# Token groups of 2, 3 and 3 tiles, one expert pipeline beside all later stages, and tensor-engine sums in the last stretch only

## The chip, the core and the metric

The kernel runs on one core of a Trainium2 chip. The metric is the device time of one execution, in microseconds (us), from the first to the last instruction of the program with what lies around it; lower is better. The core has a tensor engine (PE, with its weight loads shown as PEld), a vector engine (DVE), a scalar engine (ACT), GpSimd (POOL) and SyncE (SP). In this kernel SP issues the plain transfers and POOL the indirect ones (gathers); 16 DMA engines carry both.

## What is computed

One step of a one-layer decoder for 1024 prompt tokens and 8 sampled tokens, all in 32-bit floats, model width 1024:

```
n  = RMSNorm(x)
qa,ka,va, qb,fb,ib,gb, ga,gbr = split(n @ w_in)
oa = post(softmax(q0 k0) - lam * softmax(q1 k1)) @ va      # causal, 4 heads, two maps each
ob = HGRN2 scan over chunks of tokens, 4 heads, with its own norm and gate
h  = x + (sigmoid(ga) * (oa @ w_a) + sigmoid(gbr) * (ob @ w_b)) @ w_out
x2 = RMSNorm(h)
q  = x2 @ w_query                                          # 8 heads, two halves of 64
s1,i1 = top16(q[...,0] . keys0); s2,i2 = top16(q[...,1] . keys1)
cs,ci = top16(all sums s1 + s2); idx = 128 * i1 + i2; w = softmax(cs)
h  = h + sum over 8*16 slots of  w * gelu(x2 . expert_u[idx]) * expert_v[idx]
y  = RMSNorm(h)
```

The last part, here called the experts, needs 128 rows of `expert_u` and `expert_v` for each token. With 128 tokens to a tile, one *slot* is one such row for every token of a tile: a gather of 128 rows of 2048 numbers (8 KB, u and v side by side), a dot product with x2, a gelu, and a weighted sum into h.

## The kernel before

The 1032 tokens are nine tiles: eight of 128 prompt tokens and one of the eight sampled tokens. `GROUPS` (L47) makes two groups of them, tiles 0 to 3 (a) and 4 to 8 (b). `program` (L2267) runs a list of stages for each group, one after the other, with a barrier of all engines between stages (`Stage.end`, L161):

- `normalise` (L170), once for all tokens.
- `project` (L342): 16 column chunks of w_in with the tokens as the moving operand (L476), each chunk loaded into one of two buffers, then row blocks v, i, g with the weights as the moving operand (L488). Group b's 520 tokens go in two slices of 260.
- `attend_prompt` (L499), for b `attend_sample` (L705), `hgrn` (L898), `hgrn_out` (L1145), `merge` (L1303).
- For group a, `fronts` (L1878): for each of its four tiles h, x2, the queries and the ranking. The ranking runs on the vector engine: five passes of MAX8, FIND_INDEX8 and MATCH_REPLACE8 over 16 score lists, the same over eight lists of sums, then one-hot products that turn positions into row numbers (L1792 to L1865). Tiles 0 to 2 stay in SBUF, tile 3 is written out ("handed").

Slots are worked in two places. `Side` (L1429) works the 384 slots of tiles 0 to 2 beside all stages of group b. `SHARES` (L2339) says what percentage of them each stage takes: 18 project, 31 attend_prompt, 15 attend_sample, 20 hgrn, 3 hgrn_out, 13 merge. In each stage the engines call `side.dve(done, total)` and its like after each step of their own, and so many slots are issued there as are due. One slot is a gather on POOL (L1485), a dot product (L1556) on the vector engine, a gelu and a scaling on the scalar engine (L1498, L1500), and a sum on the vector engine two slots later (L1522). Eight ring buffers hold gathered rows; POOL waits before each gather until the sum of eight slots earlier is done.

`experts` (L1940) then works the 640 slots of tiles 3 to 7 in a loop over tiles, and eight slots for the sampled tokens behind it. Here the vector engine makes a diagonal matrix of each slot's coefficients (L2176) and the tensor engine sums, two products of 128x512 for each slot (L2073). All steps of the following tile's front (from `Front`, L1580) are placed between the slots by a list of slot numbers (`slots_with_front`), so ranking, w_out and w_query lie beside the gathers:

```
AT_H, AT_ADD, AT_ROOT, AT_N2, AT_N2T, AT_Q, AT_QN, AT_QT, AT_S = (1, 3), 5, 7, 9, 11, (13, 15), 16, 18, 20
AT_KEYS, AT_COMB, AT_BEST, AT_EXP, AT_ROWS, AT_IDX, AT_W = 23, 34, 36, 47, 49, 59, 60
```

Of the kernel before, what the change touches and what calls it, by code (L numbers as in the profile page):

```python
# [13 lines left out]
P = 128  # L20
# [30 lines left out]
GROUPS = ((0, 4), (4, NT))  # L51


N_BESIDE = 3

ARENA = 50400
# [70 lines left out]
class Group:  # L127


    def __init__(self, name, lo, hi):  # L130
        self.name, self.lo, self.hi = name, lo, hi
        self.tiles = range(lo, hi)
        self.prompt = range(lo, min(hi, NP))
        self.t0 = lo * P
        self.n = min(hi * P, T) - self.t0
        self.np = len(self.prompt) * P
        width = -(-self.n // -(-self.n // 512))
        self.slices = [(a, min(width, self.n - a)) for a in range(0, self.n, width)]
        self.sampled = hi == NT

HANDED = 2 * D + 2 * SLOTS


def parts_of(handed):
    return {"h": handed[:, 0:D], "n2": handed[:, D:2 * D], "idx": handed[:, 2 * D:2 * D + SLOTS].bitcast(U32),
            "w": handed[:, 2 * D + SLOTS:HANDED]}

# [192 lines left out]
def project(nc, top, io, c, g, side):  # L342
# [3 lines left out]
    qk, v_all, ident = c["qk"], c["v"], c["ident"]  # L346
    with ExitStack() as st:
# [4 lines left out]
        wn = [m.sb(f"wn{u}", [P, KD, 512]) for u in range(1 if g.lo else 2)]  # L352
        row_st = [m.sb(f"row_st{u}", [P, 512]) for u in range(2)]
        col_st = m.sb("col_st", [P, g.n])
        pt = [[banks.ps(f"pt{g.name}{u}_{s}", [P, 512]) for s in range(len(g.slices))] for u in range(2)]
# [21 lines left out]
        NSL = len(g.slices)  # L377
# [13 lines left out]
        def _(sp):  # L391
# [5 lines left out]
            for k in range(2, N_COLS):  # L397
                load_w(sp, k)
                if k > n_direct + 1:
                    sp.wait_ge(cols_stored, NSL * (k - 1))  # L400
                    sp.dma_start(io["hqf"][k - 2 - n_direct][:, g.t0:g.t0 + g.n], col_st).then_inc(cols_saved, 16)
            for k in range(N_COLS - 2, N_COLS):
                sp.wait_ge(cols_stored, NSL * (k + 1))
# [27 lines left out]
        def _(act):  # L431
            for k in range(N_COLS):
# [3 lines left out]
                for s, (a, n) in enumerate(g.slices):  # L436
                    dst = qk[:, k, g.t0 + a:g.t0 + a + n] if k < n_direct else col_st[:, a:a + n]
                    last = nc.scalar.copy(dst, pt[k % 2][s][:, 0:n])
                    last.then_inc(cols_stored, 1)
# [18 lines left out]
        @block.vector  # L458
        def _(dve):
            side.dve(1, 1)  # L460
# [6 lines left out]
        def _(pe):  # L467
            pe.wait_ge(xnt_landed, 16)
            for k in range(N_COLS):
                u = k % 2  # L470
                if k >= 2:
                    pe.wait_ge(cols_stored, NSL * (k - 1))
                pe.wait_ge(wt_landed[u], 16 * (k // 2 + 1))
                for d in range(KD):
                    for s, (a, n) in enumerate(g.slices):
                        last = nc.tensor.matmul(pt[u][s][:, 0:n], wt[u][:, d, :], xnt[:, d, a:a + n],  # L476
                                                start=(d == 0), stop=(d == KD - 1))
                last.then_inc(cols_done, 1)
            for n, (b, t) in enumerate(items):
# [10 lines left out]
                else:  # L490
                    pe.wait_ge(cols_stored, NSL * N_COLS)
                    c0 = CK if b == "k" else CQ
                    for h in range(H):
                        last = nc.tensor.transpose(out[0:rows(t), h * P:(h + 1) * P],
                                                   qk[:, c0 + h, t * P:t * P + rows(t)], ident[:])
                last.then_inc(rows_done, 1)


def attend_prompt(nc, top, io, c, g, side):  # L499

    qk, v_all, ident = c["qk"], c["v"], c["ident"]
    units = [(i, h) for i in g.prompt for h in range(H)]
    NG = len(g.prompt)
    with ExitStack() as st:
# [9 lines left out]
        NSC = 2 if len(g.prompt) + g.lo <= NP // 2 else 1  # L514
        sc = [[banks.ps(g.name + f"sc{b}{k}", [P, SEQ // NSC]) for k in range(2)] for b in range(NSC)]
        pt = banks.ps(g.name + "at_pt", [P, SEQ])
        o_ps = banks.ps(g.name + "o_ps", [P, H, DV])
        ot_ps = banks.ps(g.name + "ot_ps", [P, H, P])
# [19 lines left out]
        def _(pe):  # L538
            def scores(u):
                i, h = units[u]  # L540
                w = (i + 1) * P
                for k in range(2):
# [3 lines left out]
                    for k0 in range(0, w, 512):  # L546
                        n = min(512, w - k0)
                        last = nc.tensor.matmul(sc[u % NSC][k][:, k0:k0 + n],  # L548
                                                qk[k * DH:(k + 1) * DH, CQ + h, i * P:(i + 1) * P],
                                                qk[k * DH:(k + 1) * DH, CK + h, k0:k0 + n],  # L550
# [3 lines left out]
            def turn(u):  # L554
                i, h = units[u]
                pe.wait_ge(diff_ready, u + 1)
                if u >= 1:
                    pe.wait_ge(probt_ready, u)
                for b in range(i + 1):
                    last = nc.tensor.transpose(pt[:, b * P:(b + 1) * P], prob[u % 2][0][:, b * P:(b + 1) * P],  # L560
                                               ident[:])
                last.then_inc(turned, 1)

            def pv(u):
                i, h = units[u]
                pe.wait_ge(probt_ready, u + 1)
# [7 lines left out]
            def turn_out(i):  # L574
                pe.wait_ge(on_ready, i + 1)
                if i >= 1:
                    pe.wait_ge(oat_stored, i)
# [6 lines left out]
            for u in range(len(units)):  # L584
# [3 lines left out]
                pv(u)  # L588
                if u % H == 0 and u:
# [4 lines left out]
        def _(act):  # L594
            def exps(u):
                w = (units[u][0] + 1) * P
                for k in range(2):
                    q = 2 * u + k
                    act.wait_ge(neg_ready, u + 1)
                    if u >= 2:  # L600

                        act.wait_ge(turned, u - 1)
# [4 lines left out]
            def store(u):  # L607
                w = (units[u][0] + 1) * P
                act.wait_ge(turned, u + 1)
                if u >= 1:  # L610
                    act.wait_ge(pv_done, u)
                nc.scalar.copy(probt[:, 0:w], pt[:, 0:w]).then_inc(probt_ready, 1)
# [92 lines left out]
def attend_sample(nc, top, io, c, g, side):  # L705
# [5 lines left out]
    with ExitStack() as st:  # L711
# [20 lines left out]
        w_ps = banks.ps("w_ps", [P, PAGES, NS * H])  # L732
        ow_ps = banks.ps("ow_ps", [NS, NS * H])
        o_ps = banks.ps("as_o_ps", [NS * H, H, DV])
        f_ps = banks.ps("as_f_ps", [P, 512])
# [33 lines left out]
        def _(pool):  # L769
            for n in range(2 * NS):  # L770
# [14 lines left out]
                side.pool(n, 2 * NS)  # L785
            side.pool(1, 1)

        @block.tensor
        def _(pe):
            for b in range(NS):  # L790
                if b >= 1:
# [4 lines left out]
                                 ).then_inc(q_spread, 1)  # L796
            pe.wait_ge(s_ready, 1)
# [9 lines left out]
            nc.tensor.matmul(ow_ps[:], pown[:], c["sum_maps"][:], start=True, stop=True).then_inc(w_done, 1)  # L807
# [37 lines left out]
        def _(dve):  # L845
# [34 lines left out]
            link(v.tensor_copy(own_w[:], ow_ps[:]))  # L880
# [17 lines left out]
def hgrn(nc, top, io, c, g, side):  # L898
# [8 lines left out]
    with ExitStack() as st:  # L907
# [12 lines left out]
        tp = [banks.ps(g.name + f"hg_tp{b}", [P, 4, P]) for b in range(2)]  # L920
# [1487 lines left out]
```

## Time and profile before

| | us |
|---|---|
| three runs | 4554.89, 4537.21, 4544.08; median 4544.08 |
| the profiled execution, span | 4543.0 |
| vector engine busy in it | 2761.8 (61%) |
| tensor engine busy in it | 2851.9 (63%) |
| queue of the gathers, share of 16 DMA engines | 62.7% |

The span of the profiled execution is the time from its first to its last instruction; nothing else of that execution is shown, and it lies 1.1 us under the median of the three runs. A busy time is the union of an engine's instructions. The profile's slices and windows show that no engine is busy all the time: each stage has its own limit, so the rows below are cut by stage.

### The profile page before, as it was taken

What the parts mean: (1) busy time and instruction counts of PE and PEld (TensorE: products, weight loads), DVE (VectorE), ACT (ScalarE), POOL (GpSimd) and SP (SyncE); (2) the same over time, 40 slices, a digit from 0 to 9 for tenths busy, and PEclk for the clock granted to TensorE, in tenths of its full rate; (3) what the DMA queues carried; (4) which work ended last, traced back from release to release, by engine and by line L of the source; (5) the groups of instructions that cost most, each with busy time, mean ns of one, the idle gap of its engine ahead of it and who ended that gap; (6) DMA issues with size and microseconds to landing.
All of it is one profiled execution on the core that took longest, in us unless ns stands there. A gap on an engine that the chain in (4) does not pass through costs nothing. (4 is left out here: it accounts for less than half of the span.)

```text
span 4543.0 us, 27167 instructions
## 1 busy us (share of the span) xinstructions
PE 2851.9 (63%) x7469; PEld 1351.7 (30%) x7469; DVE 2761.8 (61%) x5875; ACT 770.2 (17%) x1942; POOL 1419.0 (31%) x1130
## 2 busy tenths in 40 slices
PE   6964696529722322322286676787777777778777
PEld 3432233217211110011175232332233233222222
DVE  1044114966479989799656457557646755755673
ACT  1035101101134421244233000000010000001000
POOL 0000000014345557544223234333333333342441
PEclk9976798759866655655588898988899889888987
DMA  5201422049779888988687988889989988987995
GB/s 178 84 26 32 153 75 73 10 161 349 260 305 357 343 306 324 364 314 324 223 315 314 376 344 342 339 339 353 351 320 352 367 331 341 354 343 312 348 350 216
DMA packets 228998, 1245.86 MB, mean 274 GB/s; under 512 B 26040, under 2 KB 56376, under 8 KB 95104
## 3 DMA queue, kind: packets, MB, share of 16 engines
q0 software_dynamic: 153728, 1098.98, 62.7%
q1 hardware_dynamic: 75136, 145.37, 8.9%
q8 instruction: 50, 0.82, 0.1%
q14 instruction: 84, 0.69, 0.0%
HBM read 1210.87 MB, written 33.39 MB: 274 GB/s over the span
## 5 line engine op out<-in xcount | busy, mean ns | idle before, releaser
L2073 PE MATMUL x_acc<-arena 128*128 128x512 f32 x2560 | 1334.6, 676 | 531.7 <-DVE arena L2176 531.4
L2184 DVE CUSTOM_DVE_ANT_0 arena<-arena 128x1024 f32<-128x1024 f32 x640 | 777.2, 1222 | 736.6 <-DMA arena<-in_experts,arena 727.1
L2025 POOL DMA_INDIRECT arena<-in_experts,arena x648 | 751.7, 1160 | 1250.5 <-PE x_acc L2073 1087.5
L1485 POOL DMA_INDIRECT arena<-in_experts,arena x384 | 594.5, 1548 | 1752.3 <-POOLq L163 969.0
L2073 PEld LDWEIGHTS x_acc<-arena 128*128 128x128 f32 x2560 | 531.9, 216 | 1321.2 <-DVE arena L2176 709.3
L1522 DVE SCALAR_TENSOR_TENSOR arena<-arena 128x1024 f32<-128x1024 f32 x384 | 491.3, 1280 | 127.6 <-ACT arena L1500 127.4
L1556 DVE CUSTOM_DVE_ANT_0 arena<-arena 128x1024 f32<-128x1024 f32 x384 | 467.6, 1218 | 36.4 <-DMA arena<-in_experts,arena 34.7
L2138 ACT ACTIVATE arena<-arena 128x2 f32<-128x2 f32 x320 | 65.1, 203 | 1765.0 <-DVE arena L2184 1764.9
L2176 DVE TENSOR_SCALAR arena<-ident,arena 128x128 f32<-128x128 f32 x640 | 191.2, 341 | 0.0
L476 PE MATMUL ptb<-arena 128*128 128x260 f32 x512 | 116.4, 387 | 97.2 <-DMA arena<-in_w_t 97.1
L1498 ACT ACTIVATE arena<-arena 128x1 f32<-128x1 f32 x384 | 77.3, 201 | 547.8 <-DVE arena L1556 526.4
L644 DVE TENSOR_TENSOR a_sc<-a_sc,cmask 128x128 f32<-128x128 f32 x32 | 7.9, 293 | 241.9 <-PE a_sc L548 241.9
L560 PE MATMUL b_at_pt<-ident,arena 128*128 128x128 f32 x104 | 26.4, 429 | 197.0 <-DVE arena L662 197.0
L1664 PE MATMUL x_a_ps<-arena 128*128 128x512 f32 (+1 forms) x320 | 140.6, 592 | 0.0
L1374 PE MATMUL b_mg_ps<-arena 128*128 128x260 f32 x512 | 119.4, 387 | 25.9 <-DMA arena<-in_wb 25.9
L1664 PE MATMUL a_f_a_ps<-arena 128*128 128x512 f32 x256 | 122.6, 639 | 18.2 <-DMA arena<-in_norm 13.4
L476 PEld LDWEIGHTS ptb<-arena 128*128 128x128 f32 x512 | 97.2, 191 | 116.1 <-issue 98.6
L1374 PE MATMUL a_mg_ps<-arena 128*128 128x512 f32 x256 | 115.3, 603 | 24.1 <-DMA arena<-in_wb 24.1
L488 PE MATMUL pnb<-arena 128*128 128x512 f32 (+1 forms) x240 | 109.8, 618 | 25.9 <-DMA arena<-in_w_n 25.9
L476 PE MATMUL pta<-arena 128*128 128x512 f32 x256 | 112.1, 599 | 16.7 <-DMA arena<-in_w_t 16.7
L1404 DVE TENSOR_TENSOR arena<-arena,a_mb_ps 128x512 f32<-128x512 f32 x8 | 5.5, 687 | 183.1 <-ACT arena L1389 183.1
L1500 ACT ACTIVATE arena<-arena 128x1 f32<-128x1 f32 x384 | 113.1, 295 | 12.8
(365 smaller groups left out, 3102.3 us busy)
## 6 DMA issues: line engine op xcount, KB each, us to landing
arena<-in_w_t SPq DMA_DIRECT2D x64, 512.0 KB
arena<-in_experts,arena POOLq DMA_INDIRECT x1032
arena<-in_w_n SPq DMA_DIRECT2D x6, 2048.0 KB, 12.1
arena<-in_w_out SPq DMA_DIRECT2D x2, 4096.0 KB, 12.9
arena<-in_w_query SPq DMA_DIRECT2D x2, 4096.0 KB
arena<-xnt_scratch SPq DMA_DIRECT2D x2, 2080.0 KB
arena<-in_x SPq DMA_DIRECT2D x4, 1024.0 KB
xnt_scratch<-arena SPq DMA_DIRECT2D x8, 512.0 KB, 4.2
```

The costliest lines, as they stand in the source:

```text
L476: last = nc.tensor.matmul(pt[u][s][:, 0:n], wt[u][:, d, :], xnt[:, d, a:a + n], start=(d == 0), stop=(d == KD - 1))
L488: last = nc.tensor.matmul(out[0:rows(t), :], xnt[:, d, a:a + rows(t)], wn[u][:, d, :], start=(d == 0), stop=(d == KD - 1))
L1374: nc.tensor.matmul(g_ps[q % 2][x][:, 0:n], wg[u][x][:, d, :], xnt[:, d, t0:t0 + n], start=(d == 0), stop=(d == KD - 1))
L1485: pool.indirect_dma_start(out=c["ring"][:, s0 % RING, :], out_offset=None, in_=self.io["experts"], in_offset=bass.IndirectOffsetOnAxis(ap= ...
L1500: act.activation(c["coef"][:, r], c["dots"][:, r], ACT.Copy, scale=c["first_w"][:, i, s0:s0 + 1]).then_inc(self.coef_ready, 1)
L1522: dve.scalar_tensor_tensor(out=h, in0=c["ring"][:, r, D:2 * D], scalar=c["coef"][:, r:r + 1], in1=h, op0=ALU.mult, op1=ALU.add).then_inc(s ...
L1556: dve.tensor_tensor_reduce(out=u, in0=u, in1=c["first_n2"][:, i, :], scale=1.0, scalar=0.0, op0=ALU.mult, op1=ALU.add, accum_out=c["dots"] ...
L1664: last = self.nc.tensor.matmul(self.a_ps[0:R, n * 512:(n + 1) * 512], lhs[:, k, 0:R], rhs[:, k, n * 512:(n + 1) * 512], start=(k == 0), st ...
L2025: nc.gpsimd.indirect_dma_start(out=ring[:, r, :], out_offset=None, in_=io["experts"], in_offset=bass.IndirectOffsetOnAxis(ap=rows_at, axis ...
L2073: last = nc.tensor.matmul(acc[:, n * 512:(n + 1) * 512], diag[:, s % RING, :], ring[:, s % RING, D + n * 512:D + (n + 1) * 512], start=(s ...
L2176: v.tensor_scalar(diag[:, s % RING, :], ident[:], gel[:, s % RING:s % RING + 1], w_cur[:, s:s + 1], ALU.mult, ALU.mult).then_inc(diag_read ...
L2184: ins = v.tensor_tensor_reduce(out=ring[:, r, 0:D], in0=ring[:, r, 0:D], in1=n2_cur[:], scale=1.0, scalar=0.0, op0=ALU.mult, op1=ALU.add, ...
```

## The change

Groups become tiles 0 and 1 (a, 256 tokens), 2 to 4 (b, 384) and 5 to 8 (c, 392), each in one slice. w_in, w_a, w_b, w_out and w_query are therefore read once for each of three groups. `fronts` and `experts` are gone. Each group gets two more stages: `hidden` (h and x2 for all its tiles, w_out in 16 chunks of 256 KB) and `rank` (w_query in eight chunks, then the same ranking passes, 20 steps to a tile, in the same order). h, x2, row numbers and weights of every tile are written out to `handed`. The sampled tokens' eight slots get a stage of their own, `experts_sample`.

A single pipeline, `Experts`, works all 1024 prompt slots in order of tiles; two SBUF buffers hold a tile's h, x2, numbers and weights, loaded by POOL in front of the tile's first gather. `PLAN` gives the number of slots beside each stage: 20 in a's `rank`, once tile 0 is ranked; 282 in group b; 389 in group c; the other 333 in a stage `rest` at the end, where nothing else runs. The second number is the share of slots that the tensor engine sums: 0 beside all stages (the vector engine sums them, as `Side` did), 0.7 in `rest`. For those the scalar engine now makes the diagonal matrix. Attention's transposes use one PSUM bank instead of two, four blocks at a time, and `project` has two buffers for row-block weights in every group.

```diff
-GROUPS = ((0, 4), (4, NT))
+GROUPS = ((0, 2), (2, 5), (5, NT))
...
-SHARES = {False: {project: 32, attend_prompt: 26, hgrn: 18, hgrn_out: 2, merge: 22},
-          True: {project: 18, attend_prompt: 31, attend_sample: 15, hgrn: 20, hgrn_out: 3, merge: 13}}
+PLAN = (
+    {rank: (20, 0.0)},
+    {project: (50, 0.0), attend_prompt: (34, 0.0), hgrn: (46, 0.0), hgrn_out: (6, 0.0), merge: (36, 0.0),
+     hidden: (20, 0.0), rank: (90, 0.0)},
+    {project: (62, 0.0), attend_prompt: (60, 0.0), attend_sample: (30, 0.0), hgrn: (46, 0.0), hgrn_out: (8, 0.0),
+     merge: (46, 0.0), hidden: (25, 0.0), rank: (100, 0.0), experts_sample: (12, 0.0), rest: (NP * SLOTS, 0.7)},
+)
...
+    def pool(self, done, total):
+        pool, c = self.nc.gpsimd, self.c
+        to = self.due(done, total)
+        if to:
+            to = min(self.N, to + RING - self.PE_LAG)
+        for b in range(self.at["pool"], to):
...
+            if s == 0:
+                pool.wait_ge(self.tile_landed[i % 2], 16 * (i // 2 + 1))
+            if b >= RING:
+                if self.by_pe[b - RING]:
+                    pool.wait_ge(self.pe_used, self.pe_to[b - RING + 1])
+                else:
+                    pool.wait_ge(self.dve_used, self.dve_to[b - RING + 1])
+            pool.indirect_dma_start(
...
+            if s == self.AT_LOAD and i + 1 < NP:
+                self.load(i + 1)
...
+    def act(self, done, total):
...
+            act.wait_ge(self.dots_ready, b + 1)
+            act.activation(c["dots"][:, r], c["dots"][:, r], ACT.Gelu).then_inc(self.gel_ready, 1)
+            act.wait_ge(self.gel_ready, b + 1)
+            act.activation(c["coef"][:, r], c["dots"][:, r], ACT.Copy, scale=w).then_inc(self.coef_ready, 1)
+            if self.by_pe[b]:
+                act.wait_ge(self.coef_ready, b + 1)
+                act.activation(c["diag"][:, b % RING, :], c["ident"][:], ACT.Copy, scale=c["coef"][:, r]
+                               ).then_inc(self.diag_ready, 1)
...
+            for r in range(NR):
+                R = rows(g.lo + r)
+                for n in range(STEPS):
+                    if n < 5:
+                        keys_top(n, r, R)
+                    elif n == 5:
+                        combine(r, R)
+                    elif n < 11:
+                        best_top(n - 6, r, R)
...
+                    side.dve(*point(HP + STEPS * r + n + 1))
```

How the vector engine's order changes in the ranking: L1792, L1794 and L1796 are its MAX, MAX_INDEX and MATCH_REPLACE passes (L1643, L1645, L1647 in the changed kernel). An ISA row is a slot's dot product (its second row reads the accumulator out). Before, in the expert loop, tile 4's ranking stood like this:

```order
L1792 MAX arena<-x_s_ps 128x8 x16
L2184 ISA arena<-arena 128x1024
L2184 ISA arena 128x1
L2184 ISA arena<-arena 128x1024
L2184 ISA arena 128x1
L2176 TENSOR_SCALAR arena<-ident,arena 128x128 x2
L2184 ISA arena<-arena 128x1024
L2184 ISA arena 128x1
L2184 ISA arena<-arena 128x1024
L2184 ISA arena 128x1
L2176 TENSOR_SCALAR arena<-ident,arena 128x128 x2
L1794 MAX_INDEX arena<-arena,x_s_ps 128x8 x16
```

In the changed kernel, in the `rank` stage of group b:

```order
L1643 MAX arena<-b_rk_s 128x8 x16
L2125 ISA arena<-arena 128x1024
L2125 ISA arena 128x1
L2078 SCALAR_TENSOR_TENSOR arena<-arena 128x1024
L1645 MAX_INDEX arena<-arena,b_rk_s 128x8 x16
L2125 ISA arena<-arena 128x1024
L2125 ISA arena 128x1
L2078 SCALAR_TENSOR_TENSOR arena<-arena 128x1024
```

Four slots stood between two passes, each with a dot product and a short diagonal (two to a batch); now one slot or two, each with a dot product and a full-width sum (L2078).

The second place is POOL's queue in `rest`, with the gathers (L2003), a tile's load (L1978) and the store of a finished tile (L1983):

```order
L1875 UNCONDITIONAL_BRANCH
L2003 DMA arena<-in_experts,arena 128x2048 x71
L1978 DMA arena<-handed_scratch 128x2304
L2003 DMA arena<-in_experts,arena 128x2048 x41
L1983 DMA y<-arena 128x1024
L2003 DMA arena<-in_experts,arena 128x2048 x87
L1978 DMA arena<-handed_scratch 128x2304
```

Loads and stores of tiles, which SP issued before, now stand between the gathers, and the first gather of a tile waits for its load.

## Rows read from the trace of the kernel before

**Rows 1.** The page's part 1 (busy time of each engine) and two lines of part 2.

```profile
PE 2851.9 (63%) x7469; PEld 1351.7 (30%) x7469; DVE 2761.8 (61%) x5875; ACT 770.2 (17%) x1942; POOL 1419.0 (31%) x1130
...
DMA  5201422049779888988687988889989988987995
GB/s 178 84 26 32 153 75 73 10 161 349 260 305 357 343 306 324 364 314 324 223 315 314 376 344 342 339 339 353 351 320 352 367 331 341 354 343 312 348 350 216
```

**Rows 2.** Windows, one per stage: from:to us, length, engines' busy us (x), PEclk, DMA share, GB/s.

```profile
0.00:41.30 41.30, 11.52 (x72) 9.99 (x72) 19.35 (x38) 14.15 (x24) 5.77 (x24) 0.96 0.66 209
41.30:255.00 213.70, 197.23 (x464) 87.20 (x464) 0.00 (x0) 18.66 (x32) 0.00 (x0) 0.96 0.32 108
255.00:342.60 87.60, 51.51 (x200) 30.17 (x200) 50.16 (x152) 37.19 (x95) 0.00 (x0) 0.64 0.04 13
342.60:485.50 142.90, 60.35 (x256) 32.71 (x256) 63.38 (x136) 69.80 (x136) 0.00 (x0) 0.67 0.13 39
485.50:678.00 192.50, 167.92 (x384) 73.35 (x384) 15.82 (x24) 9.97 (x17) 0.00 (x0) 0.93 0.33 120
678.00:975.80 297.80, 142.86 (x448) 68.91 (x448) 222.94 (x856) 26.49 (x34) 0.00 (x0) 0.73 0.11 38
975.80:1297.50 321.70, 231.08 (x776) 142.23 (x776) 164.41 (x208) 52.20 (x194) 120.70 (x76) 0.86 0.85 320
1297.50:1675.00 377.50, 114.41 (x456) 76.51 (x456) 358.43 (x517) 153.24 (x365) 189.73 (x120) 0.59 0.86 336
1675.00:1909.30 234.30, 79.78 (x119) 21.34 (x119) 193.99 (x238) 39.13 (x132) 155.12 (x122) 0.59 0.87 332
1909.30:2272.40 363.10, 96.83 (x340) 46.56 (x340) 293.99 (x453) 136.40 (x340) 133.26 (x89) 0.54 0.78 285
2272.40:2477.50 205.10, 170.78 (x768) 146.89 (x768) 134.47 (x196) 76.59 (x160) 59.11 (x41) 0.92 0.81 310
2477.50:4480.00 2002.50, 1484.58 (x3116) 602.79 (x3117) 1228.07 (x3021) 128.21 (x396) 747.84 (x650) 0.89 0.89 344
4480.00:4543.00 63.00, 43.09 (x71) 13.01 (x69) 16.76 (x36) 8.17 (x17) 7.49 (x8) 0.65 0.35 142
```

**Rows 3.** Timeline, vector engine, beside the attention: start us, us, instruction.

```profile
1310.10 1.22 DVE L1556 CUSTOM_DVE_ANT_0 arena<-arena 128x1024 f32<-128x1024 f32 x1
...
1311.24 1.28 DVE L1522 SCALAR_TENSOR_TENSOR arena<-arena 128x1024 f32<-128x1024 f32 x1
1312.44 1.22 DVE L1556 CUSTOM_DVE_ANT_0 arena<-arena 128x1024 f32<-128x1024 f32 x1
```

**Rows 4.** Costliest groups of the page: busy us, mean ns | idle before, releaser.

```profile
L2184 DVE CUSTOM_DVE_ANT_0 arena<-arena 128x1024 f32<-128x1024 f32 x640 | 777.2, 1222 | 736.6 <-DMA arena<-in_experts,arena 727.1
L2025 POOL DMA_INDIRECT arena<-in_experts,arena x648 | 751.7, 1160 | 1250.5 <-PE x_acc L2073 1087.5
L1485 POOL DMA_INDIRECT arena<-in_experts,arena x384 | 594.5, 1548 | 1752.3 <-POOLq L163 969.0
```

**Rows 5.** Groups by line and form, tensor engine: the projections' two passes.

```profile
L476 PE MATMUL ptb<-arena 128*128 128x260 f32 x512 | 116.4, 387 | 97.2 <-DMA arena<-in_w_t 97.1
...
L476 PE MATMUL pta<-arena 128*128 128x512 f32 x256 | 112.1, 599 | 16.7 <-DMA arena<-in_w_t 16.7
...
L488 PE MATMUL pnb<-arena 128*128 128x512 f32 x192 | 88.9, 625 | 25.9 <-DMA arena<-in_w_n 25.9
```

**Rows 6.** DMA: the gathers' queue (packets, MB, share), and two issues (KB, us to landing).

```profile
q0 software_dynamic: 153728, 1098.98, 62.7%
...
xnt_scratch<-arena SPq DMA_DIRECT2D x8, 512.0 KB, 4.2
...
arena<-handed_scratch SPq DMA_DIRECT2D x1, 1152.0 KB, 5.1
```

**Rows 7.** Timeline, vector engine, `fronts`: first and last instruction of four tiles' ranking.

```profile
731.76 0.89 DVE L1792 MAX8 arena<-a_f_s_ps 128x8 f32<-128x128 f32 x4 [24.61 <-PE a_f_s_ps L1711]
...
970.66 0.29 DVE L1865 TENSOR_TENSOR arena<-arena 128x128 f32<-128x128 f32 x1
```

More of the change, by code:

```diff
@@ new lines, in pe, with pe_end, pe_slots @@
+    def pe(self, done, total):
+        self.pe_slots(self.due(done, total) - self.PE_LAG)
+    def pe_end(self):
+        self.pe_slots(self.N)
+    def pe_slots(self, to):
+        pe, c = self.nc.tensor, self.c
+        for b in range(self.at["pe"], to):
+            if not self.by_pe[b]:
+                continue
+            i = b // SLOTS
+            first = self.pe_to[b] == self.pe_to[i * SLOTS]
+            last = self.pe_to[b + 1] == self.pe_to[(i + 1) * SLOTS]
+            if first and i:
+                pe.wait_ge(self.acc_taken, i)
+            pe.wait_ge(self.diag_ready, self.pe_to[b + 1])
+            for n in range(2):
+                ins = pe.matmul(self.acc[:, n * 512:(n + 1) * 512], c["diag"][:, b % RING, :],
+                                c["ring"][:, b % RING, D + n * 512:D + (n + 1) * 512], start=first, stop=last)
+            ins.then_inc(self.pe_used, 1)
+        self.at["pe"] = max(self.at["pe"], to)
@@ L2319, in program @@
+        c["free"] = kept.at
+        groups = [Group("abc"[n] + "_", lo, hi) for n, (lo, hi) in enumerate(GROUPS)]
+        experts = Experts(nc, c, io, acc, [PLAN[n][build] for n, g in enumerate(groups) for build in BUILDS
+                                           if build in PLAN[n]])
+        for n, g in enumerate(groups):
             for build in BUILDS:
-                if build is attend_sample and not g.sampled:
+                if build in (attend_sample, experts_sample, rest) and not g.sampled:
@@ L2321, in program @@
                     continue
-                beside.stage(build)
-                stage(nc, build, io, c, g, beside)
-            if n:
-                beside.sems.end()
-            if not g.sampled:
-                c["free"] = kept.at
-                handed = g.hi - 1 if GROUPS[n + 1][1] == NT else None
-                stage(nc, fronts, io, c, g, handed)
-                tiles = range(g.lo, g.hi if handed is None else handed)
-                beside = Side(nc, c, io, tiles, GROUPS[n + 1][1] == NT)
@@ new lines, in program @@
+        experts.sems.end()
+BUILDS = (project, attend_prompt, attend_sample, hgrn, hgrn_out, merge, hidden, rank, experts_sample, rest)
+PLAN = (
[5 more added lines that the diff above has]
+)
```

1494 lines of the change are left out of this document (706 added, 788 removed).

## Prediction

> **What bounds the kernel now.** I read the page's shares first [rows 1]: no engine is over 63% busy in 4543.0 us, so there is no single bound and the span has to be cut. The lines of slices show why: up to slice 8 the DMA engines are mostly idle, from slice 9 on their digit is 8 or 9. The windows by stage [rows 2] give three stretches. Until 975.8 us no expert row is gathered. From there to 2477.5 (1501.7 us) group b's stages run with 384 slots beside them, 3.91 us a slot. From there on the loop works 640 slots in 2002.5 us, 3.13 each, and 63.0 us end it. Adding the windows' vector-engine times in the middle stretch gives 1145 us, 76% of it: the attention is bound by that engine (358.43 of 377.5), hgrn partly (293.99 of 363.1), `project` and `merge` by the tensor engine and by transfers (DMA share 0.85 and 0.81). In the loop the DMA share is 0.89 and the vector engine is busy for 61% only: it waits 727.1 us for gathered rows [rows 4]. The ranking of tiles 4 to 7 and the sampled tokens lies in those waits and costs little.
>
> **Prices.** A slot beside a stage costs the vector engine 2.34 us, the pitch from one dot product to the next with a sum between (1310.10 to 1312.44, [rows 3]). A slot's gather moves 128 rows of 8 KB, 1.05 MB; the gathers' queue used 62.7% of the span [rows 6], 2848 us, so at most 2.76 us of all 16 engines for each of 1032 gathers. At the loop's 344 GB/s it takes 3.05 us [rows 2]. Ranking four tiles took 731.76 to 970.95 us [rows 7], 59.8 a tile. That holds early steps of later tiles and waits; `fronts` had the vector engine busy for 222.94 us [rows 2], 56 a tile, some 3 of them early steps. I take 55 for the ranking alone, bounds 53 and 60.
>
> **Group a (256 tokens).** `normalise` stays at 41.3 [rows 2]. `project`: 213.7 with 197.23 busy; half the columns and rows, 99, plus the same 16 of start and end, plus 20, since a column chunk would take 3.5 us (half of 112.1/16, [rows 5]) and its 512 KB transfer about 4.2 [rows 6]: 135. Attention 40 (half of 87.6 is 44, the narrower half less). hgrn with its output 96, between half of 142.9 and all of it, because chains and table loads for each head don't shrink. `merge` 168/2+25 = 109. `hidden` 50: w_out's products for two tiles at 15 us, a start and a tail of 10 each. `rank`: w_query's product 35, two tiles 110, 20 slots at 2.34 (47), and 15 until the first tile's load (5.1, [rows 6]) and first gather have landed: 207. Group a: **678**, where 975.8 stood, 20 slots done.
>
> **Group b (384 tokens, 282 slots).** `project`: tensor engine 116.4·384/520 = 86 for columns plus 67 for nine row items (88.9/12 each, [rows 5]), 153, with start and a tail of slots 189; by bytes 73 MB at this stage's 320 GB/s 229; I take 205. Attention: 34 slots 80, own work 46, at the 95% of before 133, fill and drain 15: 148. Its transposes in parts of four add a handover to each unit of tiles 4 to 7, at most 1 us each, behind vector work: 0, bound 16. hgrn and output: 363.1 less 37 slots (87), one tile (20) and the sampled tokens (35, bounds 0 and 60): 221. `merge`: 170.78·384/520 = 126 plus the 34 of before is 160, by bytes 54 MB at 310 GB/s 173: 165. `hidden`: 20 slots and weights are 30 MB, 88 at about 340 GB/s; tensor engine and tail 65. `rank`: eight product steps 51, in which only 11 slots are due; then one in-order queue on the vector engine holds three tiles at 55 (165) and 79 slots (185): 401, here 398 as ranking waits are partly filled. Sum **1225**.
>
> **Group c (392 tokens, 389 slots)** by the same steps: `project` 243 (223 and 270), attention 218 (377.5/16 = 23.6 a unit, less 2.4 slots), sampled attention 185 (234.3 less 28 slots is 169; POOL now issues the last 15 expert gathers ahead of the six last cache loads, so I add 16), hgrn and output 261, `merge` 190 (163 and 207), `hidden` 105 (75 and 108), `rank` 53 + 4·55 + 91·2.34 = 486, taken as 480, `experts_sample` 80 (63.0 before, 12 slots more, its final norm beside). Sum **1762**. In b and c together 671 slots take 1570 us of the vector engine and own work some 714 (105 attention, 58 sampled, 114 hgrn, 28 merge, 392 ranking and norms, 17 sampled experts), 76% of 2987, as in the middle stretch before.
>
> **Last stretch, 333 slots.** The vector engine needs 1.2 + 0.3·1.2 = 1.5 us a slot, so transfers set the pace: bounds 2.76 (busy share) and 3.13 (whole loop); 2.9 taken, near the loop without its ranking. 966, last norm and store 10. POOL's queue now holds each tile's load, and the tile's first gather waits behind it for the landing (5.1, [rows 6]); beside stages eight gathered slots at some 4 us cover that, in the last stretch two loads cost some 6 each, 12. A finished tile's store stands 40 slots into the next tile, 20 behind its norm, and holds nothing up. Together **988**. The removed diagonals and products were off the path, as was 1334.6 us of tensor engine: nothing is credited for them. The 128x128 diagonal on the scalar engine is not in this trace; a 128x512 pass there takes 0.6 us (its copies in `project`, 18.66 us for 32), so 0.2 to 0.6, beside a 2.9 us pace: 0.
>
> Sum: 678 + 1225 + 1762 + 988 = 4653 us of a span of 4543.0; the median of the runs is 1 us above it. **Forecast 4654 us, 2.4% slower.** The gain is 298 us ahead of the gathers; the loss is that ranking seven tiles, free beside the loop's gathers, now takes 881 us for 190 slots, 4.6 each, while the stretch that is left with DMA-bound slots has an idle vector engine.
>
> [...]
>
> **Rivals.** *A, faster: slots fill the stages' waits.* If the vector engine were busy 86% of b and c instead of 76%, they would take 2284/0.86 = 2656 and the kernel 4322. It decides from 80%, where the time reaches 4521. For it: the attention reached 95%, and 881 us of ranking is one dense queue. Against it: `project` had 51%, `merge` 66%, and those are bound elsewhere. Chance 0.12. *B, no change: weights and gathers don't collide.* `project`, `merge` and `hidden` at their tensor-engine times are 189+223+160+163+60+75 = 870 instead of 996, 4527. For it: in b's columns the weights mostly kept up. Against: 310 to 320 GB/s there, near the loop's 344. Chance 0.12, half of it, with the rows' own error, beyond 0.5%. *C, slower: the ring paces the last stretch.* Each of 227 slots on the tensor engine now goes dot, gelu, scaling, diagonal, two products, POOL, with eight buffers; at 3.3 us a slot it adds 133, 4787; it decides where the chain behind a landing exceeds some 8 us, eight paces of 2.9 less 15 in flight. For it: POOL waited 1087.5 us for the tensor engine before [rows 4]. Against: it did so at a DMA share of 0.89. Chance 0.18. *D, gathers alone run faster.* With no weights beside them at the best slice's 376 GB/s [rows 1], 2.79 us a slot, 4616. Chance 0.05. [...]
>
> **How the numbers follow.** The forecast has 0.53, own range 4560 to 4770 (ranking 53 to 60, last stretch 2.76 to 3.0, `project` and `merge` between their bounds). Faster by over 0.5%, about what a measurement of this kernel can tell from no change: A, half of B, a low end of the forecast's errors, 0.20. Within 0.5%: half of B and some of the forecast, 0.10. Slower: 0.70. The range 4480 to 4830 takes in B, D and most of C and leaves out A.
>
> **What would show it.** The first gather's dot product near 575 us instead of 986; group a's end near 680, b's near 1905, c's near 3665; `rank` of b and c about 400 and 480 us with the vector engine over 90% busy and a DMA share of about 0.6; the last stretch at 2.9 us a slot, DMA share 0.9, vector engine near 55%. The forecast is wrong if b and c end before 3500 us, if ranking with slots costs less than the sum of both, or if a slot of the last stretch takes over 3.2 us.
>
> PREDICTION {"us": 4654, "low": 4480, "high": 4830, "faster": 0.20, "same": 0.10, "slower": 0.70}

## The result and the profile after

The changed kernel takes 4476.21 us (median of 4 runs, 4472.53 to 4479.68); the kernel before, timed beside it, 4549.49 (4 runs, 4537.21 to 4556.57). The ratio is 0.984, 95% interval 0.982 to 0.986: 1.6% faster, where 2.4% slower was forecast. The profiled execution has a span of 4470.8 us.

The page of the changed kernel, parts 1 to 3 in extracts, answers to [rows 1, 6]:

```profile
PE 2072.8 (46%) x5841; PEld 1043.3 (23%) x5841; DVE 3080.8 (69%) x5708; ACT 1195.0 (27%) x3247; POOL 1533.9 (34%) x1137
...
DMA  5124278778798676797878685988666699999998
GB/s 201 57 80 141 100 262 346 302 284 299 273 354 353 237 259 241 291 365 295 324 281 290 222 304 214 362 349 304 226 229 226 234 378 427 410 427 407 426 427 341
...
q0 software_dynamic: 156176, 1113.13, 64.4%
```

The end is new: between the slices of 378 and 341 GB/s six stand at 407 to 427, where no slice of before passed 376. Stage by stage, the windows of the changed kernel answer to [rows 2]. They are `project` of b, `rank` of b, `rank` of c, the last stretch whole, and its inside (from:to us, length, busy us of PE, PEld, DVE, ACT and POOL, granted clock, DMA share, GB/s):

```profile
653.10:862.30 209.20, 157.23 (x412) 80.31 (x412) 119.16 (x150) 34.76 (x128) 83.14 (x50) 0.88 0.90 351
1459.70:1866.50 406.80, 52.70 (x224) 33.75 (x224) 368.66 (x908) 58.96 (x200) 127.04 (x92) 0.56 0.71 249
3066.70:3555.40 488.70, 57.52 (x256) 35.98 (x256) 443.41 (x1149) 66.98 (x223) 156.03 (x102) 0.55 0.65 229
3619.30:4470.00 850.70, 513.18 (x908) 185.78 (x908) 550.72 (x792) 265.01 (x902) 401.53 (x332) 0.86 0.97 408
3640.00:4440.00 800.00, 497.18 (x878) 180.11 (x879) 517.91 (x748) 251.98 (x862) 386.86 (x322) 0.87 1.00 422
```

Beside the ranking the vector engine is the full one (368.66 of 406.80, 443.41 of 488.70) and the DMA share is 0.71 and 0.65; in the last stretch it is the other way round, 0.97 to 1.00 at 408 to 422 GB/s with the vector engine at 65%.

Here is the whole forecast beside the measurement. Ends are those of the last instruction of a group's stages.

| | forecast, us | measured, us |
|---|---|---|
| group a, to the end of `rank` | 678 | 652.6 |
| group b, 282 slots | 1225 | 1213 (653.1 to 1866.5) |
| group c with `experts_sample`, 389 slots | 1762 | 1752 (1867 to 3618.8) |
| last stretch, 333 slots | 988 | 851 (3619.3 to 4470) |

The three groups together missed by 46 us of 3665. Three quarters of the error, 137 us, lie in the last stretch: a slot there takes 851/333 = 2.55 us, ends included, and not 2.9. The loop of before took 3.13 for the same gather. Had its slots kept that pace, the last stretch would be 333 x (3.13 - 2.55) = 193 us longer and the change slower by about 120 us.

The rows on the gathers of the changed kernel, from 3640 to 4440 us, say what their queue waited for and how long a gather takes from its issue to its landing:

```profile
L2003 POOL DMA_INDIRECT arena<-in_experts,arena x318: 932/939/1983, 3639.5 to 4435.7; - x159
its engine sat idle before it (us, times) until:
  DVE arena L2078: 294.2, 91
...
  DMA arena<-handed_scratch: 29.3, 2
...
DMA to landing us min/median/max: 5.4/12.4/15.8
```

318 gathers in 800 us are one in 2.52 us, and a landing takes 12.4, so 12.4/2.52 = 4.9 gathers are under way on average.

### The profile page after: what moved, and what is told of

The parts are those of the page before. It is cut to its first block and busy times, and to the rows that moved or that the text cites. A ratio compares the mean times of both kernels' runs of the same rounds, so it can differ in the third digit from the quotient of the medians.

```text
span 4470.8 us, 24525 instructions
## 1 busy us (share of the span) xinstructions
PE 2072.8 (46%) x5841; PEld 1043.3 (23%) x5841; DVE 3080.8 (69%) x5708; ACT 1195.0 (27%) x3247; POOL 1533.9 (34%) x1137
## 5 line engine op out<-in xcount | busy, mean ns | idle before, releaser
L2003 POOL DMA_INDIRECT arena<-in_experts,arena x1024 | 1445.9, 1412 | 2305.4 <-DVE arena L2078 2132.7
L2078 DVE SCALAR_TENSOR_TENSOR arena<-arena 128x1024 f32<-128x1024 f32 x797 | 1019.5, 1279 | 205.6 <-ACT arena L2029 205.4
L2027 ACT ACTIVATE arena<-arena 128x1 f32<-128x1 f32 x1024 | 206.6, 202 | 1886.6 <-DVE arena L2125 1885.4
L2064 PE MATMUL e_acc<-arena 128*128 128x512 f32 x908 | 513.2, 708 | 324.7 <-ACT arena L2032 274.9
L2064 PEld LDWEIGHTS e_acc<-arena 128*128 128x128 f32 x908 | 185.8, 221 | 652.2 <-ACT arena L2032 425.7
L2029 ACT ACTIVATE arena<-arena 128x1 f32<-128x1 f32 x1024 | 301.5, 294 | 33.2
L458 PE MATMUL ptc<-arena 128*128 128x392 f32 x256 | 94.5, 528 | 243.0 <-DMA arena<-in_w_t 242.8
L458 PE MATMUL ptb<-arena 128*128 128x384 f32 x256 | 93.6, 526 | 181.7 <-DMA arena<-in_w_t 181.7
L1599 PE MATMUL c_rk_s<-arena 64*128 64x128 f32 (+1 forms) x128 | 13.2, 387 | 220.8 <-DVE zero L1657 220.2
L1346 PE MATMUL c_mg_ps<-arena 128*128 128x392 f32 x256 | 89.3, 502 | 37.2 <-DMA arena<-in_wa 37.2
L1346 PE MATMUL b_mg_ps<-arena 128*128 128x384 f32 x256 | 87.7, 495 | 28.1 <-DMA arena<-in_wa 28.1
L2032 ACT ACTIVATE arena<-ident,arena 128x128 f32<-128x128 f32 x227 | 91.1, 401 | 7.4
```

What stands on the lines that cost most here:

```text
L458: last = nc.tensor.matmul(pt[u][:, 0:g.n], wt[u][:, d, :], xnt[:, d, :], start=(d == 0), stop=(d == KD - 1))
L1346: nc.tensor.matmul(g_ps[z][:, 0:g.n], wg[u][:, d, :], xnt[:, d, :], start=(d == 0), stop=(d == KD - 1))
L1599: last = nc.tensor.matmul(s_ps[0:R, x, k, :], qt[s, k, r * P:r * P + R], keys[s, k, :], start=True, stop=True)
L2003: pool.indirect_dma_start(out=c["ring"][:, r, :], out_offset=None, in_=self.io["experts"], in_offset=bass.IndirectOffsetOnAxis(ap=self.til ...
L2027: act.activation(c["dots"][:, r], c["dots"][:, r], ACT.Gelu).then_inc(self.gel_ready, 1)
L2029: act.activation(c["coef"][:, r], c["dots"][:, r], ACT.Copy, scale=w).then_inc(self.coef_ready, 1)
```

## Experiments

Two theories of the 2.55 us. **Places:** the loop of before wasn't paced by transfers at all. Its gathers waited for free buffers of the ring of eight, which dot product, gelu, diagonal and product, in batches of two, held so long that the DMA engines ran short; the new pipeline frees a buffer sooner. **Sums:** what counts is which engine sums, the vector engine having been relieved, or loaded, by the split of 0.7. The count that ties the first theory together: if all places are always taken, places x pace = landing + holding, where holding is the time from a row's landing to its buffer's release.

### Who sums in the last stretch

```diff
-     merge: (46, 0.0), hidden: (25, 0.0), rank: (100, 0.0), experts_sample: (12, 0.0), rest: (NP * SLOTS, 0.7)},
+     merge: (46, 0.0), hidden: (25, 0.0), rank: (100, 0.0), experts_sample: (12, 0.0), rest: (NP * SLOTS, 0.0)},
```

> From the changed kernel; no slot of the last stretch is summed by the tensor engine (share 0.0 for 0.7). The vector engine then needs 2.34 us a slot, still under the 2.47 us that 128 packets of 8 KB at 309 ns take on 16 engines. Theory P: the vector engine and the transfers are both nearly full, 2.5 to 2.7 us a slot, the stretch 840 to 900. Theory S: without tensor products it gets faster or stays, 820 to 851.

The second run has 1.0 in the same place.

> From the changed kernel; the tensor engine sums nearly all slots of the last stretch (share 1.0 for 0.7). Theory P: the same number of places, so 2.5 to 2.65 us a slot, the stretch within 30 us of 851. Theory S: with the sums on the tensor engine, as in the loop before, the pace goes back towards the loop's 2.95 to 3.1 us, the stretch to 970 to 1030.

Measured, in one run each: 4479.0 us with the vector engine alone, 4466.89 with the tensor engine for all slots that may go there; before, on that chip, 4555.08. Windows inside the last stretch, of the first run and then of the second:

```profile
3640.00:4440.00 800.00, 0.00 (x0) 0.00 (x0) 771.21 (x965) 163.67 (x642) 539.65 (x323) 0.50 1.00 421
```

```profile
3640.00:4430.00 790.00, 607.46 (x1225) 211.91 (x1224) 404.06 (x648) 284.29 (x940) 311.79 (x318) 0.97 1.00 422
```

The vector engine is busy for 96% in one and 51% in the other, the DMA share is 1.00 in both, and the rate stays at 421 and 422 GB/s. The last stretch is paced by transfers, as forecast; the tensor engine's part in it is worth nothing that can be measured. By the count, a place was held for 8 x 2.52 - 15.1 = 5.0 us after the landing with the tensor engine alone (its landing stands in the last section), where the changed kernel, with its share of 0.7, has 8 x 2.52 - 12.4 = 7.8: buffers came back sooner, more gathers were under way, and the pace stayed.

### Fewer places in the last stretch

```diff
+            held = 6
+            if b >= self.N - 325:
+                if self.by_pe[b - held]:
+                    pool.wait_ge(self.pe_used, self.pe_to[b - held + 1])
+                else:
+                    pool.wait_ge(self.dve_used, self.dve_to[b - held + 1])
```

> From the changed kernel; in the last stretch alone POOL also waits until the slot six places back (not only eight) has been summed, so two ring buffers stay empty. Theory P (places in flight): the last stretch ran at 2.55 us a slot because 5.05 gathers were in flight on the mean; the loop of the kernel before had 2.9 of them and 3.13 us. Two places less leave about 3 in flight, and the stretch goes from 851 us to 980 to 1060 (2.95 to 3.2 us a slot), DMA share 0.8 to 0.9; the kernel about 4600 to 4680. Theory S (who sums): the pace came from fewer products on the tensor engine, the diagonals off the vector engine and no ranking; buffers don't matter, the stretch stays within 20 us of 851.

The second run has 5 for 6.

> As the run with six places, but five: theory P expects some 2 gathers in flight, 3.6 to 4.4 us a slot, a last stretch of 1180 to 1450 us and a DMA share of 0.55 to 0.7. Theory S expects no change from 851 us.

Measured, in one run each: 4568.57 us with six places and 4683.77 with five, 96 and 211 us of span over the changed kernel. Windows inside the last stretch with six places, and then its gathers with their landing:

```profile
3650.00:4530.00 880.00, 534.26 (x872) 191.71 (x870) 513.55 (x741) 249.30 (x853) 360.95 (x320) 0.82 0.97 380
```

```profile
L2009 POOL DMA_INDIRECT arena<-in_experts,arena x316: 932/938/1953, 3653.0 to 4529.2; - x158
...
DMA to landing us min/median/max: 5.3/9.0/12.5
```

The same two views with five:

```profile
3650.00:4630.00 980.00, 557.62 (x847) 191.62 (x848) 500.74 (x724) 243.70 (x834) 335.97 (x310) 0.79 0.88 333
```

```profile
L2009 POOL DMA_INDIRECT arena<-in_experts,arena x306: 934/941/1987, 3655.9 to 4624.5; - x153
...
DMA to landing us min/median/max: 5.4/8.0/11.2
```

The direction is that of places, the size smaller than expected. The count holds: holding is 8 x 2.52 - 12.4 = 7.8 us with eight places, 6 x 2.78 - 9.0 = 7.7 with six (316 gathers in 880 us) and 5 x 3.20 - 8.0 = 8.0 with five (306 in 980). It is the same chain each time, and what places are left after it feed the DMA engines. With five, 8.0/3.20 = 2.5 gathers are under way, and the row reads as the loop of before did: a DMA share of 0.88 and 333 GB/s, for 0.89 and 344 in [rows 2].

### The kernel before with a quicker release

```diff
-    BATCH = 2
+    BATCH = 1
...
-            return [(12 + at * 52 // NB, step) for at, step in front]
+            return [(12 + at * 52 // 64, step) for at, step in front]
...
-                    if at == b:
+                    if 2 * at + 1 == b:
```

The last two lines keep the ranking steps of the next tile at the slots where they stood.

> From the kernel before; slots of its loop go one by one instead of in pairs (batch of 1 for 2), the steps of the ranking keep their places between the slots. Theory P: a buffer comes free up to one slot earlier on each link of the chain dot, gelu, diagonal, product, so 3.4 to 4.5 gathers are in flight instead of 2.9 and the loop's 640 slots take 1650 to 1850 us instead of 2002; the kernel 4200 to 4400. Theory S: the same engines do the same work, the loop stays within 40 us of 2002.

Measured: 4258.59 us (2 runs), 0.936 of before, interval 0.933 to 0.939. The DMA view of 2600 to 4100 us, before:

```profile
GB/s 356 327 353 322 343 370 334 349 310 354 313 347 358 342 354 362 355 342 354 268 360 314 365 371 340 372 369 360 367 269 355 310 354 333 376 349 354 329 353 352
...
q0 software_dynamic: 70182, 511.00, 87.7%
q1 hardware_dynamic: 5047, 4.81, 1.0%
...
arena<-in_experts,arena POOLq DMA_INDIRECT x486
```

With batches of one:

```profile
GB/s 395 382 423 421 422 396 423 366 422 386 421 421 421 420 422 350 352 421 382 421 422 421 416 421 353 345 420 383 422 421 422 417 417 400 310 412 380 419 419 421
...
q0 software_dynamic: 82129, 598.10, 97.1%
q1 hardware_dynamic: 5184, 5.31, 1.1%
...
arena<-in_experts,arena POOLq DMA_INDIRECT x572, 11.8
```

The same loop, gathers and ranking between the slots: 572 gathers for 486, at up to 423 GB/s. The same dot products, diagonals and sums are done; each slot goes through the chain by itself and gives its buffer back by itself. That the buffers are what counts in this, and not a finer order of the work, is for the next run to show. The loop, up to where the last tile's sum is taken into h, went from 2004.5 us (2477.5 to 4482.0) to 1716.8 (2478.7 to 4195.5), 288 less, as the whole kernel:

```profile
4482.01 1.22 DVE L2195 TENSOR_TENSOR arena<-x_acc,arena 128x1024 f32<-128x1024 f32 x1 [6.71 <-PE x_acc L2073]
```

```profile
4195.49 1.23 DVE L2195 TENSOR_TENSOR arena<-x_acc,arena 128x1024 f32<-128x1024 f32 x1 [3.44 <-PE x_acc L2073]
```

A gather takes 2.62 us instead of 3.09, and a place is held for 8 x 2.62 - 11.8 = 9.2 us. For before the profile gives no landing; with 8.2, between 8.0 at a pace of 3.20 and 8.4 at 2.88 (next run), it is 8 x 3.09 - 8.2, some 16.5 us, an estimate.

### The count put to the test

```diff
-                    if s % BATCH == 0 and not (first and s < RING):
+                    if not (first and s < HELD):
...
-                        hold(pool, slot_used, i * NB + (s - RING) // BATCH + 1, pool_held)
+                        hold(pool, slot_used, i * NB + s - HELD + 1, pool_held)
```

This is the kernel before with batches of one and `HELD = 6`.

> The kernel before with batches of one, and in its expert loop a gather that waits for the slot six back instead of eight. If the loop is set by places, places x pace = landing + holding. With batches of one the trace has a pace of 2.62 us (572 gathers in 1500 us) and a landing of 11.8, so a place is held for 8 x 2.62 - 11.8 = 9.2 us after the landing. At six places, with the landing between 9.0 at 2.78 and 8.0 at 3.20 (the runs of the changed kernel with six and with five places), the count closes at a pace of 2.95 with a landing of 8.5: 640 x 0.33 = 211 us more than that kernel's 4255.5, 4420 to 4510, landing 8 to 9 us, DMA share of the gathers' queue near 0.9. If batches of one helped for another reason (a finer order on the engines) and places don't matter there, the time stays within 30 us of 4255.5.

Measured: 4407.53 us (one run; before 4551.72), 150 us of span over eight places. The DMA view of 2600 to 4100 us:

```profile
q0 software_dynamic: 74802, 544.73, 91.8%
...
arena<-in_experts,arena POOLq DMA_INDIRECT x520, 8.4
```

1500/520 = 2.88 us a gather for 2.95 expected, landing 8.4 for 8.5, holding 6 x 2.88 - 8.4 = 8.9 for 9.2. The total lies 12 us under the range given: 640 times the difference of the paces, 0.26, is 166, nearer to the 150 measured than my 211.

### The ranking stages

```diff
-     hidden: (20, 0.0), rank: (90, 0.0)},
+     hidden: (20, 0.0), rank: (0, 0.0)},
...
-     merge: (46, 0.0), hidden: (25, 0.0), rank: (100, 0.0), experts_sample: (12, 0.0), rest: (NP * SLOTS, 0.7)},
+     merge: (46, 0.0), hidden: (25, 0.0), rank: (0, 0.0), experts_sample: (12, 0.0), rest: (NP * SLOTS, 0.7)},
```

> From the changed kernel; no slots beside the ranking of groups b and c, the last stretch takes those 190 as well. If ranking and slots simply add on the vector engine (2.34 us a slot): the two rank stages fall from 407 and 489 us to about 205 and 265, the last stretch grows by 190 times 2.55 = 485, and the kernel is 40 to 110 us slower than 4471. If the slots had filled waits of the ranking instead (rival A of the prediction), the rank stages fall by much less, under 150 us each, and the kernel gets over 150 us slower.

The other run keeps the slots and has 0.9 for 0.0 in both.

> From the changed kernel; beside the ranking of groups b and c the tensor engine sums 0.9 of the slots. If the vector engine's queue is the limit there, a slot costs it 1.14 us instead of 2.34: 171 slots at 1.2 less is 205 us, the two rank stages 310 and 380 us, the kernel about 4270. If the tensor engine's low clock in this stretch, the scalar engine or the gathers limit it, the stages fall by under 100 us together.

Measured: 4530.21 us without slots (one run; 58 of span over the changed kernel) and 4339.32 with 0.9 (2 runs; 0.954 of before, 0.950 to 0.957). Windows of the first run, `rank` of b and of c and the last stretch:

```profile
1452.10:1666.30 214.20, 53.27 (x224) 34.03 (x224) 159.31 (x633) 6.05 (x12) 0.00 (x0) 0.62 0.07 24
2862.10:3130.40 268.30, 57.34 (x256) 35.92 (x256) 212.08 (x844) 6.42 (x13) 0.00 (x0) 0.60 0.06 19
3191.40:4527.50 1336.10, 827.60 (x1428) 299.40 (x1428) 863.96 (x1244) 417.28 (x1418) 630.78 (x526) 0.84 0.98 412
```

Of the second, `rank` of b and of c:

```profile
1457.80:1797.70 339.90, 222.44 (x528) 96.15 (x528) 278.45 (x833) 90.19 (x278) 120.12 (x92) 0.82 0.78 298
3006.80:3417.50 410.70, 253.07 (x600) 105.61 (x600) 341.17 (x1064) 102.06 (x311) 148.47 (x102) 0.81 0.74 272
```

Alone, the stages take 214 and 268 us; my sum had 51 + 165 = 216 and 53 + 220 = 273. Slots add (406.8 - 214.2)/90 = 2.14 us and (488.7 - 268.3)/100 = 2.20 each. The forecast charged 2.34, but for 79 and 91 of them only, 2.05 and 2.13 over all. In vector-engine time a slot adds (368.66 - 159.31)/90 = 2.33 and (443.41 - 212.08)/100 = 2.31. So nearly all of it lengthens the stage, 0.1 to 0.2 us fills waits, and rival A has little ground. With the tensor engine they add 1.40 and 1.42. A slot moved out of `rank` costs 2.55 in the last stretch, so leaving 190 of them out loses some 0.38 x 190 = 72 us, 58 as measured, while relieving the vector engine pays 67 and 78 us. That is less than the 205 us I had expected of it: a slot was to cost 1.14, and what makes it 1.40 wasn't separated (the vector engine is busy for 82% and 83% there).

### The tensor engine beside all stages

Here 0.9 stands for 0.0 in every stage of groups b and c but `experts_sample`.

> The changed kernel with the tensor engine given nine tenths of the sums (0.9 for 0.0) in every stage of groups b and c, at the same number of slots in each. Giving it the two ranking stages alone took 133 us off (4338.1 of span for 4470.8). If the vector engine sets the other stages too (its busy share there was 0.90 beside attention of prompts, 0.83 beside hgrn, 0.65 beside attention of the sample), each slot taken off it gives back about what it gave in rank, 0.74 us (67 us for 90 slots and 78 for 100): 34 + 60 of attention 70 us, 46 + 46 of hgrn 68 us, 30 of the sample up to 22 us, and the whole comes to 4180 to 4260. If those stages are set by their own chains or by the transfers, they keep their lengths and the whole stays at 4320 to 4350; if the tensor engine's own work in them is delayed by the sums, they lengthen and it is above 4350. The last stretch keeps its 850 us in every case.

The second run also changes three numbers of slots in group c.

```diff
-    {project: (62, 0.9), attend_prompt: (60, 0.9), attend_sample: (30, 0.9), hgrn: (46, 0.9), hgrn_out: (8, 0.9),
+    {project: (62, 0.9), attend_prompt: (70, 0.9), attend_sample: (36, 0.9), hgrn: (50, 0.9), hgrn_out: (8, 0.9),
```

> As the run with nine tenths everywhere, and twenty more slots in group c: attention of prompts 70 for 60, attention of the sample 36 for 30, hgrn 50 for 46. If those stages have room once the vector engine is relieved, the last stretch is shorter by 20 x 2.55 = 51 us and the stages grow by less, so 20 to 50 us under the run without the twenty. If a slot costs a stage as much as the last stretch, no difference (within 10 us).

Measured: 4575.88 us (10 runs; 1.002 of before, 1.000 to 1.004) and 4579.16 (10 runs). The gain of `rank` is lost and more: `project` of b went from 209 to 258 us, of c from 240 to 297, `merge` from 159 to 212 and from 179 to 241, `hidden` from 84 to 100 and from 101 to 127. `project` of b in the first run:

```profile
650.50:908.20 257.70, 225.87 (x584) 111.96 (x584) 69.18 (x107) 52.00 (x172) 55.34 (x50) 0.93 0.77 285
```

The tensor engine's busy time rose by 69 us to 88% of the stage, and the DMA share fell from 0.90 to 0.77. Where that engine has a stage's own work, sums beside it are paid for; whether by the time of the sums or by their place in its queue wasn't separated. Attention of b, that of the sample and hgrn became 7 to 11 us shorter, not the 22 to 34 I had allowed, and attention of c 8 us longer: the vector engine alone doesn't set them. Twenty more slots made no difference, the second case.

The last run of this group gives the tensor engine sums only where it was idle (lines of the changed kernel's `PLAN`):

```diff
+    {project: (50, 0.0), attend_prompt: (34, 0.9), hgrn: (46, 0.9), hgrn_out: (6, 0.0), merge: (36, 0.0),
+     hidden: (20, 0.0), rank: (98, 0.9)},
+    {project: (62, 0.0), attend_prompt: (60, 0.0), attend_sample: (30, 0.9), hgrn: (46, 0.9), hgrn_out: (8, 0.0),
+     merge: (46, 0.0), hidden: (25, 0.0), rank: (112, 0.9), experts_sample: (12, 0.0), rest: (NP * SLOTS, 0.7)},
```

> The changed kernel with the tensor engine given nine tenths of the sums only in the stages whose own work leaves it idle (granted clock 0.50 to 0.64 there): attention of prompts in b, attention of the sample, hgrn and rank in b and c; project, merge, hidden and hgrn_out stay with the vector engine, and the ranking stages take 98 and 112 slots for 90 and 100. Against the run with the ranking stages alone (4338.1 of span): the run with nine tenths everywhere had attention in b 8 us shorter, the sample 9, hgrn 8 and 12, so 37 us; the 20 slots moved into rank cost 1.4 us each there ((410.7 - 268.3)/100) and save 2.55 in the last stretch, 23 us. So 4270 to 4300. If the stalls of the run with nine tenths everywhere came from the tensor engine's turn in any stage, and not only in those that load it themselves, it is above 4340.

Measured: 4258.56 us (4 runs, 4248.02 to 4265.39), 0.936 of before, interval 0.934 to 0.938; it beats both kernels and does a little better than expected. The kernel before with batches of one reaches the same time by another way. A kernel that joins the two wasn't tried.

## Why the prediction was wrong

**The failed step** is the price of the last stretch: "so transfers set the pace: bounds 2.76 (busy share) and 3.13 (whole loop); 2.9 taken, near the loop without its ranking". It measured 2.55 with its ends and 2.52 inside. That transfers set the pace there held, shown by the runs with 0.0 and 1.0. But the loop of before, from which I took the price, wasn't paced by them: a DMA share of 0.89 [rows 2] stood beside gathers that waited for buffers, and 344 GB/s lies between what so few gathers drew in the runs, 333 with 2.5 under way (five places) and 367 with 2.9 (`HELD = 6`, 2600 to 4100 us). Giving buffers back one by one instead of in pairs showed it in that kernel (2.62 us a gather for 3.09), and five places made the same row in the changed one. The row that spoke was on the page: POOL idle for 1250.5 us ahead of the loop's gathers, 1087.5 of it for the tensor engine's release of a buffer [rows 4]. I used it in rival C against the new chain and dismissed it "at a DMA share of 0.89".

**The lower bound was no bound.** 2.76 us came from the queue's busy share over the whole span. Now the queue has 0.644 x 4470.8 = 2879 us for 1032 gathers and the few other loads, 2.79 each, while the inside of the last stretch shows 2.52 at a share of 1.00. So gathers beside the stages carry some (2879 - 333 x 2.52)/699 = 2.9 us, an estimate. Other traffic isn't needed for that. In the last stretch itself, at one and the same work, share times length is 1.00 x 800/318 = 2.52 us for each gather with eight places, 0.97 x 880/316 = 2.70 with six and 0.88 x 980/306 = 2.82 with five; in the loop of before it is 0.877 x 1500/486 = 2.71 in pairs and 0.971 x 1500/572 = 2.55 one by one. So the busy time that a gather is charged is itself larger when fewer are under way, and it is no floor for the pace.

**Rivals.** C was wrong in its sense and right in its count: the chain behind a landing takes 7.8 us, just inside the 8 at which it would decide. The 15 us in flight that I set stood in no row, it was my estimate; with all places taken the landing is what is left, 12.4; the runs with fewer places show where C begins. D had the right direction and the wrong cause and size: it put the gain down to the absence of weights, but from 2600 to 4100 us the plain transfers took 1.0% of the DMA engines in the loop of before, and the same loop with batches of one went faster beside 1.1%. And 376 GB/s was the best slice of a kernel that ran short of places. The price that held was in the packets of that same trace: the median 8 KB packet of its gathers took 309 ns, as in the changed kernel, so the 128 of a gather take 128 x 309/16 = 2.47 us of all 16 engines, and gathers that overlap came to 2.52 at 422 GB/s inside the last stretch. At 2.47 us the sum of the forecast would be 4510, and with the groups' 46 us 4464, against 4470.8. A is out: the vector engine was busy for 77% of groups b and c, where A needed 80 and the forecast had 76, and in `rank` slots were added nearly in full. The window of both groups:

```profile
653.10:3618.80 2965.70, 1234.06 (x3641) 625.89 (x3641) 2288.22 (x4193) 808.75 (x2075) 1093.73 (x753) 0.67 0.78 289
```

B is out by what `project`, `merge` and `hidden` of b and c measured, 972 us together for 996 in the forecast and 870 in B.

**What was right.** The groups: `project` 122.7, 209.2 and 240.4 us for 135, 205 and 243; attention 41.7, 137.8, 220.8 for 40, 148, 218; hgrn with its output 93.1, 213.5, 260.8 for 96, 221, 261; `merge` 98, 158.8, 178.6 for 109, 165, 190; `hidden` 46.3, 83.8, 100.8 for 50, 88, 105; `rank` 205.8, 406.8, 488.7 for 207, 398, 480; attention of the sample 194.6 for 185; `experts_sample` 62.9 for 80. `rank` had the vector engine at 91% and a DMA share of 0.65 to 0.71. The first dot product came at 550.9 us, for 575. The loss that I described is there: ranking with slots takes 406.8 + 488.7 = 895 us for 190 slots. The two tiles' loads were put at 12 us. POOL waited 29.3 us for them; as gathers were still under way through most of that, the transfers lost less. In the 40 slices of 20 us from 3640 to 4440 us, two lie low, those at 3800 and 4120 us, where POOL waits for the loads that it issued at 3788.9 and 4113.4:

```profile
GB/s 427 427 427 426 427 428 428 426 331 427 428 427 427 426 428 426 427 428 428 427 425 428 427 427 311 428 426 427 427 427 428 427 426 427 428 427 428 426 426 427
```

(427 - 331)/427 x 20 = 4.5 us and (427 - 311)/427 x 20 = 5.4 us, some 10 together: the term held.

## What to carry to other kernels

A DMA share near 0.9 didn't make a stretch transfer-bound here: at 0.89 in the loop of before and 0.88 with five places the gathers waited for buffers. Look whether the queue that issues waits for free buffers, and set places x pace against landing + holding; that the rate is that of the transfers was shown where a quicker release changed nothing (5.0 us of holding for 7.8, 422 GB/s in both). A price taken from a stretch that is short of places was no bound for one that isn't (3.13 us in the loop of before, 2.55 in the last stretch), and neither was the queue's busy time divided by its transfers: it fell from 2.82 to 2.52 us as places went from five to eight. Give an idle engine sums where it is idle in that stage, not by its mean over the kernel: the tensor engine was busy for 46% of the changed kernel, but for 13% and 12% of `rank` of b and c (52.70 of 406.8, 57.52 of 488.7) and for 75% of `project` of b (157.23 of 209.2), and the same 0.9 took 67 and 78 us off the two ranking stages and added 16 to 62 to those with matrix products of their own.

## What the runs showed of the hardware

- A gather of 128 rows of 8 KB lands 5.2 us after its issue at the least (the whole trace of the changed kernel), and in 12.4 when gathers follow at 2.52 us. About five under way filled all 16 DMA engines (share 1.00, 422 GB/s); 6.0 of them (15.1/2.52, all sums on the tensor engine, landing below) gave no more, 3.2 gave 380 GB/s and 2.5 gave 333.
- POOL's own time to issue a gather was longer beside a busier vector engine: a median of 939 ns with it at 65%, but 1777 ns with it at 96%; which of its instructions does it wasn't separated. The issue stayed within the pace of 2.5 us, so it cost nothing here. The gathers' row inside the last stretch with all sums on the vector engine, and then the landing with all on the tensor engine:

```profile
L2003 POOL DMA_INDIRECT arena<-in_experts,arena x319: 935/1777/1939, 3639.9 to 4439.6; - x160
```

```profile
DMA to landing us min/median/max: 5.4/15.1/16.5
```

- The granted clock in `rank` of b was 0.56 with 52.70 us of tensor work in 406.8 and 0.82 with 222.44 in 339.9: the clock's records in the trace are at 0.5 or at 1.0 of full speed, and with sums beside it more of the stage was at 1.0. What this gave back to the stage's own products wasn't separated.
